# Early ring fills, a norm beside the sample index, and reordered projection openings in a two-layer decoder step

## The chip, the cores and the metric

The kernel runs on one core of a Trainium2 chip. The time is the device time of one execution in microseconds (us); 1 us is 1000 ns. Five engines run their own instruction streams: PE (matrix products and transposes; PEld is its weight load), DVE (vector work), ACT (activations, copies), POOL and SP, which here mostly issue transfers (DMA). They meet through semaphores. SBUF holds the tiles, eight banks of PSUM take PE's results.

## The reference

One inference step of two layers for a prompt of 1024 tokens and for 8 samples of 4 new tokens, each sample with 2048 past tokens in paged caches (128 tokens a page). Model width is 1024, all in float32.

```python
# layer 0: native sparse attention (compressed, selected, window) and a gated linear recurrence
y = concat([o_a * silu(z_a), o_b * silu(z_b)]) @ w_out;  x = x + gate * y
# layer 1: differential attention with a norm per head, and attention over the top 256 of an index
attn = p[..., 0, :] - lam * p[..., 1, :];  o = einsum('btghs,bsgd->btghd', attn, v)
o_c = _rmsnorm(o_c, subln_g) * (1.0 - DIFF_LAMBDA_INIT)
score = einsum('bth,bths->bts', wib * IDX_HEADS ** -0.5, relu(idx_s));  top_k(score, 256)
y = concat([o_c * silu(z_c), o_d * silu(z_d)]) @ w_out;  x = x + gate * y
```

A final RMSNorm with its own gain gives the outputs. The new key and value rows are outputs too.

## The kernel before

Each layer runs as a row of stages, and each stage is one or more blocks in which every engine has its own program; a block ends when all engines have ended. The order of the instructions on an engine is the order in which the code writes them. In each layer the stages are: norm, input projection (`project`), prompt attention (`attend_pairs`), sample attention, output projection (`output_projection`).

*Layer 0.* `nsa_prompt` begins with a small block (from line 1616) in which POOL clears a tile, ACT copies the sample rows and DVE compresses keys and values. The long attention block follows. In `nsa_sample` (line 2292) POOL fills a `Ring` of ten slots of 1 MB: 16 units of the compressed cache by indirect gather (line 2041, row numbers from the tile `rows`), ten pieces of layer 1's ada weights (line 2046), 16 units of the selected cache, 8 half units of window state and 6 more ada pieces. Before a slot is filled again POOL waits until PE has released it. DVE multiplies each compressed unit by the weights `cmp_w` (line 2354), PE sums the blocks (line 2375), copies follow (line 2341). PE multiplies ada pieces (line 350) between the steps that choose blocks, and then turns the selected keys (line 2143), scores them (line 2173) and so on, four units of four samples a half.

*Layer 1.* `diff_prompt` ends with a block for the norm per head: squares on ACT (line 1744), sums, root and scaling on DVE (lines 1754 to 1763); then `mix_prompt`: PE turns the normed rows into banks 0 to 3 (line 1578), DVE multiplies them into `mix` (line 1593). Then `sample_index`: POOL gathers 16 runs of index keys (line 2676), PE turns them in banks 5 and 6 (line 2691), ACT copies (line 2744), PE multiplies by the queries (line 2721) into banks 0 to 3, DVE rectifies (line 2785), PE sums over heads (line 2705) and DVE places the scores (line 2779). After `dsa_prompt`'s attention `layer1_sample` fills a ring of eleven slots with 16 units of diff keys, 16 of diff values and 16 of dsa keys and values, and turns and scores them as above.

*Output projection.* 18 units of 24 products (line 2894; a unit is 128 rows and one half of the columns, 512). The weights are loaded in quarters of 1 MB, two per half of the columns. ACT rounds a quarter (line 2961), DVE computes the rest (line 2908), and splits `mix` alike (lines 174, 175) for each row tile. Gates of prompt and samples are spread over partitions by PE (lines 2873, 2874) and copied by DVE (lines 2929, 2930); in layer 1 the final gain is too (lines 2880, 2935). SP loads the second half's quarters into the same room once DVE has read the first half's, and then x. The first unit's result waits for x (line 2948).

```python
                for u in range(NU):
                    ring.gather(pool, t["cmp_cache"], u)
                for n in range(m.EARLY):
                    m.fill(pool, n)
...
                split_mix(0)
                split_mix(1)
                dve.wait_ge(spread, 1)
```

## Time and profile before

| | |
|---|---|
| Median of 3 runs | 2036.73 us (2033.31 to 2038.12) |
| Profiled execution | 2032.63 us, span 2030.8 us |
| PE busy | 1759.9 us, 87% of the span |
| DVE busy | 1114.6 us, 55% |
| ACT busy | 694.5 us, 34% |
| POOL busy | 173.8 us, 9% |
| Moved by DMA | 188.68 MB, mean 93 GB/s |

The span runs from the first to the last instruction of the profiled execution. A timeline row gives start, length, engine, line, operation, output and inputs and how many instructions are merged in it; in brackets stand the idle time of that engine just before and what ended it. A wait row gives a total over a window, the number of waits and the longest. A window row gives the window, its length, busy time and instructions of PE, PEld, DVE, ACT and POOL, then the granted clock of PE as a share of full speed (2.4 GHz), the mean busy share of the DMA engines, and GB/s. `PEq`, `SPq` and `POOLq` are the engines' own sequencers; as a releaser they stand mostly for a block's end.

### The profile page before, as it was taken

The numbers are of one execution on the slowest core, as the hardware profiler recorded it, in microseconds if no ns is written. First come the engines' busy times: TensorE is split into PE (matmuls) and PEld (weight loads), VectorE is DVE, ScalarE is ACT, GpSimd is POOL, SyncE is SP. The second block draws the span as 40 slices with busy tenths as digits, with TensorE's granted clock in tenths as the row PEclk, the third lists the DMA queues.
The fourth block names the chain that finished last, engine by engine and source line by source line (L and its number), as shares of the span: only waits on it lengthen the run. The fifth ranks groups of instructions, "written<-read, shape, count | busy, mean of one in ns | idle before, by whom it ended". The sixth has DMA issues, their size and how long they took to land. (4 is left out here: it accounts for less than half of the span.)

```text
span 2030.8 us, 29356 instructions
## 1 busy us (share of the span) xinstructions
PE 1759.9 (87%) x11653; PEld 1258.7 (62%) x11653; DVE 1114.6 (55%) x2257; ACT 694.5 (34%) x1763; POOL 173.8 (9%) x212
## 2 busy tenths in 40 slices
PE   3799999699999677599899999998876999687698
PEld 2699999566666345377766766664554566444376
DVE  2445401377776733344213999943984997333454
ACT  3535521366655012211223211104662666222211
POOL 1000100000000631200000100000002000332000
PEclk9899999799999887899999999998997999899799
DMA  7411010000000993541201201100003000986221
GB/s 256 166 52 65 33 62 26 1 1 1 1 2 1 364 405 146 229 158 52 73 35 41 75 22 43 43 22 1 1 1 84 1 1 2 370 354 270 94 106 55
DMA packets 36248, 188.68 MB, mean 93 GB/s; under 512 B 5964, under 2 KB 6061, under 8 KB 19535
## 3 DMA queue, kind: packets, MB, share of 16 engines
q0 software_dynamic: 19632, 119.64, 15.1%
q1 hardware_dynamic: 16480, 67.16, 9.0%
q8 instruction: 94, 1.54, 0.3%
q14 instruction: 42, 0.34, 0.1%
HBM read 171.82 MB, written 19.12 MB: 94 GB/s over the span
## 5 line engine op out<-in xcount | busy, mean ns | idle before, releaser
L917 PE MATMUL banks<-hT,w_in 128*128 128x352 f32 x864 | 256.5, 459 | 0.0
L917 PEld LDWEIGHTS banks<-hT,w_in 128*128 128x128 f32 x864 | 164.0, 190 | 90.7
L2894 PE MATMUL banks<-w_out_parts,mix_parts 128*128 128x512 f32 (+1 forms) x864 | 202.5, 397 | 14.8 <-DVE w_out_parts L2908 10.5
L2894 PEld LDWEIGHTS banks<-w_out_parts,mix_parts 128*128 128x128 f32 (+1 forms) x864 | 158.0, 183 | 60.1 <-issue 12.1
L1529 ACT ACTIVATE nsa_p<-banks,nsa_negmax 128x512 f32<-128x512 f32 (+3 forms) x192 | 104.1, 556 | 93.9 <-DVE nsa_negmax L1446 93.9
L912 PE MATMUL banks<-hT_high,w_in_high 128*128 128x352 f32 x384 | 125.3, 326 | 0.0
L912 PE MATMUL banks<-hT_rest,w_in_high 128*128 128x352 f32 x384 | 124.0, 323 | 0.0
L912 PE MATMUL banks<-hT_high,w_in_rest 128*128 128x352 f32 x384 | 123.9, 323 | 0.0
L1446 DVE TENSOR_REDUCE nsa_negmax<-banks 128x2 f32<-128x1024 f32 (+4 forms) x77 | 84.6, 1099 | 69.5 <-PE banks L1398 59.3
L914 PE MATMUL banks<-w_in,hT 128*128 128x256 f32 (+3 forms) x576 | 117.4, 357 | 1.2 <-PEq L654 1.2
L914 PEld LDWEIGHTS banks<-w_in,hT 128*128 128x128 f32 (+1 forms) x576 | 92.2, 181 | 24.2 <-issue 10.6
L1413 PE MATMUL banks<-cf,nsa_p 128*128 128x128 f32 x544 | 77.9, 284 | 16.1 <-ACT nsa_pT L1370 13.1
L1972 DVE TENSOR_SCALAR_CACHE_REDUCE dsa_mask<-mix,prompt_top_bits 128x384 bf16<-128x384 f32 (+2 forms) x102 | 89.7, 942 | 0.6
L1413 PEld LDWEIGHTS banks<-cf,nsa_p 128*128 128x128 f32 x544 | 60.7, 145 | 36.4 <-issue 19.2
L1034 ACT ACTIVATE mix<-banks 128x352 f32<-128x352 f32 x48 | 22.2, 464 | 175.9 <-PE banks L917 91.2
L1972 DVE TENSOR_SCALAR_CACHE_REDUCE dsa_mask<-prompt_top_upper,prompt_top_bits 128x384 bf16<-128x384 bf16 (+2 forms) x90 | 79.2, 942 | 0.5
L2143 PE MATMUL banks<-cf,l_ring 128*128 128x128 f32 x384 | 61.5, 301 | 20.1 <-DMA l_ring<-in_diff_k_cache,rows 7.9
L1446 DVE TENSOR_REDUCE diff_negmax<-banks 128x2 f32<-128x1024 f32 (+3 forms) x38 | 44.3, 1165 | 60.3 <-PE banks L1398 58.8
L801 DVE TENSOR_TENSOR w_in_rest<-w_in,w_in_high 128x2048 fp32r<-128x2048 f32 (+1 forms) x10 | 23.1, 2306 | 97.4 <-ACT w_in_high L796 97.3
L907 PE MATMUL banks<-w_in_high,hT_high 128*128 128x264 f32 (+1 forms) x216 | 67.3, 312 | 8.8 <-DVE hT_rest L947 8.8
L1529 ACT ACTIVATE dsa_p<-banks,dsa_negmax 128x512 f32<-128x512 f32 (+3 forms) x96 | 54.7, 580 | 52.8 <-DVE dsa_negmax L1446 52.8
L912 PEld LDWEIGHTS banks<-hT_high,w_in_high 128*128 128x128 f32 x384 | 72.1, 188 | 0.5
(568 smaller groups left out, 3405.4 us busy)
## 6 DMA issues: line engine op xcount, KB each, us to landing
w_in<-in_w_in SPq DMA_DIRECT2D x24, 1056.0 KB, 4.9
nsa_ring<-in_ada POOLq DMA_DIRECT2D x16, 1024.0 KB, 14.7
ada_w<-in_ada SPq DMA_DIRECT2D x8, 1024.0 KB, 17.6
w_out<-in_l_w_out SPq DMA_DIRECT2D x8, 1024.0 KB, 6.7
x_in<-in_x_prompt SPq DMA_DIRECT2D x2, 2048.0 KB, 24.7
nsa_ring<-in_state_l_win_kv POOLq DMA_DIRECT2D x8, 512.0 KB, 7.5
x_after<-in_x_prompt SPq DMA_DIRECT2D x1, 4096.0 KB, 15.8
x_mid<-x_after SPq DMA_DIRECT2D x8, 512.0 KB, 2.6
```

The source lines that it names most:

```text
L801: eng.tensor_tensor(w_rest[:, j % slots, :, 0:width(j)], v, w_high[:, j % slots, :, 0:width(j)].bitcast(F32), ALU.subtract).then_inc(w_spl ...
L907: last = pe.matmul(bank[0:rows, 0:n], lhs, rhs, start=a == 0 and x == 0, stop=a == KT - 1 and x == 2)
L912: last = pe.matmul(bank[:, 0:cn], lhs, rhs, start=a == 0 and x == 0, stop=a == KT - 1 and x == 2)
L914: last = pe.matmul(bank[0:rows, 0:n], k.hT[:, a, r0:r0 + rows], w[:, j % slots, a, 0:n], start=(a == 0), stop=(a == KT - 1))
L917: last = pe.matmul(bank[:, 0:cn], w[:, j % slots, a, m * P:(m + 1) * P], k.hT[:, a, c0:c0 + cn], start=(a == 0), stop=(a == KT - 1))
L1034: act.activation(k.mix[:, what + m, c0:c0 + cn], k.bank[i % 4][:, 0:cn], ACT.Silu).then_inc(free[i % 4], 1)
L1413: last = pe.transpose(k.bank[4 + c % 2][:, i * P:(i + 1) * P], p_sb[:, u % SLOTS, col:col + P], k.const("ident"))
L1446: last = dve.tensor_reduce(of_unit(nm, u), scores_of(u), X, ALU.max, negate=True)
L1529: last = act.activation(slot_of(u)[:, g, x], scores_of(u)[:, g, x], ACT.Exp, bias=of_unit(nm, u)[:, g, x:x + 1], accum_out=of_unit(rs, u)[ ...
L1972: last = dve.tensor_scalar(m, v, threshold(j), None, op, ALU.add, accum_out=seen[:, j:j + 1])
L2143: last = pe.transpose(o[:, j * P:(j + 1) * P], ring.run[:, g % ring.slots, c % 2 * 4 + j, k_col[m]:k_col[m] + P], k.const("ident"))
L2894: last = pe.matmul(k.bank[u % 4][0:n, :], lhs, rhs, start=a == 0 and x == 0, stop=a == KT - 1 and x == 2)
```

## The change

1. The sample rings are made earlier. In layer 0 five of the ten slots lie in room that is free during the prompt attention, and POOL gathers the first five compressed units in that attention's small opening block. In layer 1 six of the eleven slots (four in the room of tensors that diff attention alone uses, two in room of their own) are filled at the start of dsa attention, with the first six units of diff keys. The sample stages fill the rest in the order as before.
2. The norm per head of diff attention, its product into `mix` and the copies of the sample rows are no longer blocks of their own. A class `DiffNorm` issues them inside `sample_index`'s block, with two tiles for squares in place of eight and three banks (2, 3, 4) in place of four.
3. In layer 1 the first half of the projection's weights is loaded by POOL as the last two fills of the ring, into the slots that the projection then reads.
4. In both output projections DVE computes the first two quarters' rests right behind the first split of `mix`; PE spreads the sample gates behind the first unit and the final gain behind the second.

```diff
--- before.py
+++ after.py
@@ -232,15 +232,23 @@
                     if layer == 0:
+                        k.ring = Ring(k, "nsa_ring", 10).add(k.sb(samples, "nsa_ring_held", [P, 5, KEYS, 2 * P], side="right"))
                         nsa_prompt(k)
                     else:
+                        k.held_stack = k.choice_stack = ExitStack()
                         diff_prompt(k)
                         dsa_prompt(k)
                 k.give_back_semaphores()
+                k.stage_sems += k.ring.filled + k.ring.free
+                if layer == 1:
+
+                    k.sb(x_stack, "w_out1", [P, 2, KEYS, 2 * P])
+                    k.w_out = k.early[:, 0:2]
...
@@ -259,10 +267,15 @@
+        k.ring = Ring(k, "l1_ring", 11)
+        k.early = k.under("l1_ring_first", [P, 4, KEYS, 2 * P], F32)
         k.qT = k.sb(st, "qcT", [P, 4, R])
+        k.kT = {n: k.sb(st, f"{n}_T1", [P, R]) for n in ("dk0", "dk1")}
+        k.v = {"dv": k.sb(st, "dv_v", [P, RT, 2 * P])}
...
@@ -1376,6 +1389,11 @@
         with nc.Block() as block:
+            if prefetch is not None:
+                @block.gpsimd
+                def _(pool):
+                    prefetch(pool)
+
@@ -1616,6 +1634,7 @@
                     pool.memset(k.qb["nsa"][:, :, :, :], 0.0).then_inc(cleared, 1)
+                    k.ring.follow(pool, nsa_items(k), 5)
...
@@ -1725,43 +1744,77 @@
         attend_pairs(k, "diff", jobs, values, close, scale, maps=True)
         with ExitStack() as ws:
...
-        mix_prompt(k, "diff", out, 0, k.lam[:, 6:7])
+            k.sample_score = k.sb(k.choice_stack, "idx_score_s", [P, QUARTER + NS], side="right")
+            sample_index(k, DiffNorm(k, ws, out))
+
+
+class DiffNorm:
+    BANKS = (2, 3, 4)
...
+    def squares(self, act):
+        for i in range(SEQ // P):
+            if i >= 2:
+                act.wait_ge(self.reduced, i - 1)
+            act.activation(self.square[:, i % 2, :], self.out[:, i, :], ACT.Square).then_inc(self.squared, 1)
...
+    def normalise(self, dve):
+        k = self.k
+        k.dve_order.link(dve, dve.tensor_scalar(k.lam[:, 6:7], k.vec[:, 8:9], 1.0 - LAM_INIT, None, ALU.mult))
+        dve.wait_ge(self.root, 1)
+        k.dve_order.link(dve, dve.reciprocal(self.ss[:, :, :], self.ss[:, :, :]))
+        for i in range(SEQ // P):
+            o = self.heads(self.out[:, i, :])
+            dve.tensor_tensor(o, o, self.ss[:, i, :].unsqueeze(2).to_broadcast([P, 4, P]), ALU.mult).then_inc(self.normalised, 1)
...
+    def turn(self, pe, u):
+        m, g = self.units[u]
+        pe.wait_ge(self.normalised, 4 * g + 4)
+        if u >= len(self.BANKS):
+            pe.wait_ge(self.taken, u - len(self.BANKS) + 1)
...
@@ -1854,10 +1907,10 @@
         with ExitStack() as ws:
-            k.sample_score = k.sb(ws, "idx_score_s", [P, QUARTER + NS], side="right")
-            sample_index(k)
             k.index_stack.close()
-            attend_pairs(k, "dsa", jobs, values, close, scale_heads, dve_copies=None, beside=SampleChoice(k, ws, k.bank[7]))
+            k.ring.add(k.early[:, 2:4]).add(k.sb(k.held_stack, "l1_ring_held", [P, 2, KEYS, 2 * P], side="right")).add(k.early[:, 0:2])
+            attend_pairs(k, "dsa", jobs, values, close, scale_heads, dve_copies=None, beside=SampleChoice(k, ws, k.bank[7]),
+                         prefetch=lambda pool: k.ring.follow(pool, layer1_items(k), 6))
...
@@ -2036,24 +2099,45 @@
+    def follow(self, pool, items, count=None):
+
+        for cache, u in items[self.issued:count]:
+            self.gather(pool, cache, u)
...
+    def load_w_out(self, pool, layer):
+        for c in range(2):
+            i = self.next(pool)
+            pool.dma_start(self.slot(i).rearrange("p i n -> p (i n)").rearrange("p (a n) -> p a n", n=512), self.k.t[f"l{layer}_w_out"].rearrange(
+                "(a p) n -> p a n", p=P)[:, c * KT // 2:(c + 1) * KT // 2, 0:512]).then_inc(self.filled[i], 16)
...
@@ -2587,12 +2671,8 @@
-                for s in range(2):
-                    for cache in ("diff_k_cache", "diff_v_cache"):
-                        for u in joint_units()[8 * s:8 * s + 8]:
-                            ring.gather(pool, t[cache], u)
-                for u in joint_units():
-                    ring.gather(pool, t["dsa_cache"], u)
+                ring.follow(pool, layer1_items(k))
+                ring.load_w_out(pool, 1)
@@ -2711,7 +2793,11 @@
                         turn(n)
+                        if n >= NU // 2:
+                            norm.turn(pe, n - NU // 2)
                     pe.wait_ge(copied, first + GROUP)
+                    if first == DB:
+                        pe.wait_ge(norm.taken, len(norm.units))
@@ -2737,11 +2823,16 @@
+                norm.squares(act)
                 for n in range(NU):
+                    if n == 4:
+                        norm.roots(act)
...
+                act.wait_ge(norm.cleared, 2)
+                keep_sample_rows(k, act, 1)
@@ -2752,6 +2843,7 @@
                 link(dve.memset(qz[:, :, :], 0.0))
+                norm.reduce(dve)
@@ -2766,6 +2858,8 @@
                 link(dve.tensor_scalar(wsum[:, :], wsum[:, :], 0.5 * HD ** -0.5, None, ALU.mult))
+                norm.normalise(dve)
+                norm.mix(dve)
@@ -2842,7 +2938,7 @@
-                for h in range(2):
+                for h in range(layer, 2):
@@ -2870,15 +2966,22 @@
                 for h in range(2):
-                    pe.matmul(k.bank[4 + h][:, :], k.const("gate_prompt"), k.gate9s[layer][:, h * 512:(h + 1) * 512], start=True, stop=True)
-                    last = pe.matmul(k.bank[6 + h][0:NS, :], k.const("gate_sample"), k.gate9s[layer][:, h * 512:(h + 1) * 512], start=True, stop=True)
+                    last = pe.matmul(k.bank[4 + h][:, :], k.const("gate_prompt"), k.gate9s[layer][:, h * 512:(h + 1) * 512], start=True, stop=True)
...
+                def beside(u):
+                    if u == 0:
+                        for h in range(2):
+                            last = pe.matmul(k.bank[6 + h][0:NS, :], k.const("gate_sample"), k.gate9s[layer][:, h * 512:(h + 1) * 512],
+                                             start=True, stop=True)
+                        last.then_inc(spread, 1)
+                    elif u == 1 and layer == 1:
...
+                    beside(u)
@@ -2923,20 +3027,22 @@
                 split_mix(0)
+                rest_of_w(0)
                 split_mix(1)
...
-                rest_of_w(0)
-                rest_of_w(1)
@@ -2957,7 +3063,10 @@
-                        act.wait_ge(loaded[h][c], 16)
+                        if h == 0 and layer == 1:
+                            k.ring.landed(act, k.ring.issued - 2 + c)
+                        else:
+                            act.wait_ge(loaded[h][c], 16)
```

On POOL, in layer 0 from the prompt attention's opening block on; `cmp_cache` is the compressed cache, `nsa_ring` the ring, `nsa_ring_held` the slots that exist early. Before, and then of the change:

```order
L1618 MEMSET nsa_qb 128x256
L154 ISA
L2041 DMA nsa_ring<-in_cmp_cache,rows 128x2048 x16
L2046 DMA nsa_ring<-in_ada 128x2048 x10
L2041 DMA nsa_ring<-in_sel_cache,rows 128x2048 x6
```

```order
L1636 MEMSET nsa_qb 128x256
L2109 DMA nsa_ring_held<-in_cmp_cache,rows 128x2048 x5
L154 ISA x2
L2109 DMA nsa_ring<-in_cmp_cache,rows 128x2048 x5
L2109 DMA nsa_ring_held<-in_cmp_cache,rows 128x2048 x5
L2109 DMA nsa_ring<-in_cmp_cache,rows 128x2048
L2114 DMA nsa_ring<-in_ada 128x2048 x4
L2114 DMA nsa_ring_held<-in_ada 128x2048 x5
L2114 DMA nsa_ring<-in_ada 128x2048
L2109 DMA nsa_ring<-in_sel_cache,rows 128x2048 x4
```

Five gathers stand ahead of the row `ISA`, which lies between the two stages; the other eleven, and all that follows them, keep their order.

On DVE, from the last copy of diff attention to the sample index's first rectified scores; `diff_ss` holds the sums of squares, `qi_z` and `wi_` rows prepare the index's queries and weights, `ki_relu` are the rectified scores. Before, and then of the change:

```order
L1724 COPY diff_out<-banks 128x512
L1754 TENSOR_REDUCE diff_ss<-diff_square 128x4 x8
L1756 TENSOR_SCALAR diff_ss<-diff_ss 128x32
L1758 TENSOR_SCALAR lam<-vec 128x1
L1760 RECIPROCAL diff_ss<-diff_ss 128x32
L1763 TENSOR_TENSOR diff_out<-diff_out,diff_ss 128x512 x8
L1593 SCALAR_TENSOR_TENSOR mix<-banks,lam,mix 128x512 x8
L2750 TENSOR_TENSOR wi_diagonal<-cf,wi 32x32 x4
L2753 MEMSET idx_score_s 96x32
L2754 MEMSET qi_z 128x256
L2760 COPY qi_z<-qiT 64x4x4 x16
L2765 TENSOR_TENSOR wi_picked<-banks,cf 128x128
L2767 TENSOR_REDUCE wi_sum<-wi_picked 128x32
L2768 TENSOR_SCALAR wi_sum<-wi_sum 128x32
L2785 TENSOR_SCALAR ki_relu<-banks 128x512 x2
```

```order
L1743 COPY diff_out<-banks 128x512
L2841 TENSOR_TENSOR wi_diagonal<-cf,wi 32x32 x4
L2844 MEMSET idx_score_s 96x32
L2845 MEMSET qi_z 128x256
L1783 TENSOR_REDUCE diff_ss<-diff_square 128x4 x8
L1785 TENSOR_SCALAR diff_ss<-diff_ss 128x32
L2852 COPY qi_z<-qiT 64x4x4 x16
L2857 TENSOR_TENSOR wi_picked<-banks,cf 128x128
L2859 TENSOR_REDUCE wi_sum<-wi_picked 128x32
L2860 TENSOR_SCALAR wi_sum<-wi_sum 128x32
L1793 TENSOR_SCALAR lam<-vec 128x1
L1795 RECIPROCAL diff_ss<-diff_ss 128x32
L1798 TENSOR_TENSOR diff_out<-diff_out,diff_ss 128x512 x8
L1817 SCALAR_TENSOR_TENSOR mix<-banks,lam,mix 128x512 x8
L2879 TENSOR_SCALAR ki_relu<-banks 128x512 x2
```

The index's preparation now stands ahead of the norm's scaling and of the product into `mix`, and the scores come behind all of it.

On DVE, at the opening of the last projection; `w_out_parts` holds the weights' two parts, `gate_rows` and `gate_rows_s` the gates, `y` a unit's result. Before, and then of the change:

```order
L174 CAST mix_parts<-mix 128x1024
L175 TENSOR_TENSOR mix_parts<-mix,mix_parts 128x1024
L174 CAST mix_parts<-mix 128x1024
L175 TENSOR_TENSOR mix_parts<-mix,mix_parts 128x1024
L2929 COPY gate_rows<-banks 128x512
L2930 COPY gate_rows_s<-banks 32x512
L2929 COPY gate_rows<-banks 128x512
L2930 COPY gate_rows_s<-banks 32x512
L2935 COPY final_g<-banks 128x512 x2
L2908 TENSOR_TENSOR w_out_parts<-w_out,w_out_parts 128x2048 x4
L2948 TENSOR_TENSOR y<-banks,gate_rows 128x512
```

```order
L174 CAST mix_parts<-mix 128x1024
L175 TENSOR_TENSOR mix_parts<-mix,mix_parts 128x1024
L3012 TENSOR_TENSOR w_out_parts<-l_ring_first,w_out_parts 128x2048 x2
L174 CAST mix_parts<-mix 128x1024
L175 TENSOR_TENSOR mix_parts<-mix,mix_parts 128x1024
L3034 COPY gate_rows<-banks 128x512 x2
L3038 COPY gate_rows_s<-banks 32x512 x2
L3012 TENSOR_TENSOR w_out_parts<-l_ring_first,w_out_parts 128x2048 x2
L3043 COPY final_g<-banks 128x512 x2
L3054 TENSOR_TENSOR y<-banks,gate_rows 128x512
```

Two of the four weight instructions moved from behind the gates and the final gain to behind the first split, and they read the ring's slots.

## Rows read from the trace of the kernel before

**Rows 1.** Window in layer 0 samples: engines' busy, PEclk, DMA share, GB/s.

```profile
674.00:742.00 68.00, 50.51 (x492) 27.58 (x492) 49.01 (x87) 4.33 (x11) 41.15 (x31) 0.89 1.01 417
```

**Rows 2.** Timeline, that stage opens: start, length, engine, line, work [idle <-releaser].

```profile
664.45 0.35 SPq L2507 DMA_DIRECT2D cmp_w<-in_cmp_w  x1
...
673.07 4.71 DVE L2354 TENSOR_TENSOR nsa_ring<-nsa_ring,cmp_w 128x2048 f32<-128x2048 f32 x2 [7.49 <-DMA nsa_ring<-in_cmp_cache,rows]
```

**Rows 3.** Tile cmp_w: from its load's issue to its landing.

```profile
DMA to landing us min/median/max: 5.3/5.3/5.3
```

**Rows 4.** Waits of PE, 717 to 742 us: total, times, longest.

```profile
PE banks L350 <- DMA nsa_ring<-in_ada: 2.0, 2, 1.4
```

**Rows 5.** Waits, 742 to 770 us, selected attention's first half.

```profile
PE banks L2143 <- DMA nsa_ring<-in_sel_cache,rows: 5.6, 4, 1.9
```

**Rows 6.** Timeline, POOL there: gathers before and beside line 2354, direct loads.

```profile
666.79 0.97 POOL L2041 DMA_INDIRECT nsa_ring<-in_cmp_cache,rows  x1 [0.30 <-issue]
...
689.57 2.23 POOL L2041 DMA_INDIRECT nsa_ring<-in_cmp_cache,rows  x1 [0.30 <-issue]
...
701.99 2.22 POOL L2046 DMA_DIRECT2D nsa_ring<-in_ada  x4
```

**Rows 7.** Timeline, the prompt attention's small opening block and what follows it.

```profile
372.75 0.31 POOL L1618 MEMSET nsa_qb<- 128x256 f32 x1 [135.40 <-POOLq L832]
...
384.05 1.22 PE L1390 MATMUL banks<-sel_T,qT 64*128 64x128 f32 x8 [4.76 <-PEq L1615]
```

**Rows 8.** Windows: norm, its product into mix, sample index.

```profile
1518.00:1530.00 12.00, 0.02 (x1) 0.06 (x1) 10.33 (x20) 8.27 (x21) 0.77 (x2) 0.66 0.00 0
1530.00:1537.50 7.50, 6.34 (x32) 6.10 (x32) 5.83 (x8) 0.00 (x0) 0.00 (x0) 0.63 0.01 2
1537.50:1569.30 31.80, 22.09 (x170) 12.18 (x170) 9.24 (x35) 9.45 (x16) 15.21 (x16) 0.79 0.48 133
```

**Rows 9.** Timeline, sample index: first gather and first turn.

```profile
1538.42 1.01 POOL L2676 DMA_INDIRECT ki_run<-in_kidx_cache,rows  x1 [19.37 <-SPq L2669]
...
1541.82 1.12 PE L2691 MATMUL banks<-cf,ki_run 128*128 128x128 f32 x4 [2.12 <-DMA ki_run<-in_kidx_cache,rows]
```

**Rows 10.** Timeline, PE, layer 1 samples: key turns, first scores, both halves.

```profile
1733.63 1.97 PE L2143 MATMUL banks<-cf,l_ring 128*128 128x128 f32 x8 [5.42 <-DMA l_ring<-in_diff_k_cache,rows]
...
1749.53 1.92 PE L2173 MATMUL banks<-l_kt,diff_qb 128*32 128x512 f32 x16
...
1785.51 3.29 PE L2143 MATMUL banks<-cf,l_ring 128*128 128x128 f32 x20
...
1796.79 1.92 PE L2173 MATMUL banks<-l_kt,diff_qb 128*32 128x512 f32 x16
```

**Rows 11.** Waits of PE, 1727 to 1750 us: total, times, longest.

```profile
PE banks L2143 <- DMA l_ring<-in_diff_k_cache,rows: 7.9, 4, 5.4
```

**Rows 12.** Timeline, opening of the last projection.

```profile
1906.33 2.04 PE L2873 MATMUL banks<-gate,cf 128*128 128x512 f32 x2 [2.73 <-PEq L2587]
...
1911.55 1.91 ACT L2961 ACTIVATE w_out_parts<-w_out 128x2048 fp32r<-128x2048 f32 x1 [7.22 <-DMA w_out<-in_l_w_out]
...
1918.53 4.49 DVE L2908 TENSOR_TENSOR w_out_parts<-w_out,w_out_parts 128x2048 fp32r<-128x2048 f32 x2
...
1920.97 23.72 PE L2894 MATMUL banks<-w_out_parts,mix_parts 128*128 128x512 f32 x96 [3.80 <-DVE w_out_parts L2908]
...
1940.75 0.69 DVE L2948 TENSOR_TENSOR y<-banks,gate_rows 128x512 f32<-128x512 f32 x1 [6.51 <-DMA x_after<-x_mid]
...
1946.73 76.72 PE L2894 MATMUL banks<-w_out_parts,mix_parts 128*128 128x512 f32 x336 [2.04 <-DVE mix_parts L175]
```

**Rows 13.** Window, first matmuls of the last projection.

```profile
1921.00:1925.00 4.00, 4.00 (x10) 3.20 (x11) 2.03 (x1) 0.00 (x0) 0.00 (x0) 0.55 0.73 246
```

**Rows 14.** Timeline, opening of the layer 0 projection.

```profile
859.00 5.81 DVE L2908 TENSOR_TENSOR w_out_parts<-w_out,w_out_parts 128x2048 fp32r<-128x2048 f32 x2 [0.39 <-ACT w_out_parts L2961]
...
888.87 6.45 PE L2894 MATMUL banks<-w_out_parts,mix_parts 128*128 128x512 f32 x20 [2.35 <-DVE mix_parts L175]
```

More of the change, by code:

```diff
@@ L446, in multiply @@
             pe.wait_ge(self.finished, 1)
-        self.columns(pe, self.bank_of(n), ring.run[:, u % ring.slots]).then_inc(self.product, 1)
+        self.columns(pe, self.bank_of(n), ring.slot(u)).then_inc(self.product, 1)
         pe.wait_ge(self.product, n + 1)
@@ L2511, in _ @@
             def _(pool):
-                for u in range(NU):
-                    ring.gather(pool, t["cmp_cache"], u)
+                ring.follow(pool, nsa_items(k)[0:NU])
                 for n in range(m.EARLY):
@@ L2671, in _ @@
             def _(pool):
+                pool.memset(k.qb["diff"][:, :, :, :], 0.0).then_inc(norm.cleared, 1)
+                pool.memset(k.qb["dsa"][:, :, :, :], 0.0).then_inc(norm.cleared, 1)
                 for n, (half, b) in enumerate(order):
```

137 lines of the change are left out of this document (78 added, 59 removed).

## The prediction

> **What bounds the kernel now.** I read the page first: TensorE (PE) is busy for 87% of the span, but that is a mean over stages. Then the windows of the five places that the change touches, the waits inside them, and the timeline where a wait ends. The prompt attentions and input projections keep PE full and move almost no data; the change adds gathers beside them and leaves their own work alone. The time to be had lies in stretches where PE waits.
>
> In layer 0's sample stage the DMA engines are the limit: from 674 to 742 us their share is 1.01 at 417 GB/s [rows 1], so 1 MB (1.049e6 bytes) lands every 2.51 us. VectorE (DVE) starts line 2354 only when the first ring units are there [rows 2], and PE still waits for ring units of ada weights and of selected keys later [rows 4, 5]. Between diff attention and dsa attention stand 51.3 us in three blocks, in none of which any engine is full [rows 8]. In layer 1's sample stage the first 16 key turns take 15.90 us where the second half's take 11.28 [rows 10]. In the last projection PE begins 14.64 us after the block does, behind the load of the weights and a queue of DVE copies [rows 12].
>
> **The change, part by part.** The sums are made against the profiled execution's own 2032.63 us (span 2030.8 and 1.8 around it), which lies 4.1 below the median of the runs shown.
>
> *Layer 0 ring, five units early.* Line 2354 now starts at 673.07, 8.6 us after the stage's load of cmp_w is issued [rows 2]. That load takes 5.3 us [rows 3] and is still needed, so the earliest new start is 664.45 + 5.3 = 669.8: 3.2 us won. With five units of 1 MB gone from a saturated stretch, 5 x 2.51 = 12.6 us of transfers are no longer ahead of the ada and selected units; the PE waits that rows 4 and 5 count, 2.0 and 5.6, lie in that backlog and should go. Sum 10.8, taken as 11. The second half of the selected attention waits for slots that the first half frees, which the change leaves, so nothing is won there. Bounds: 3.2 (only the start moves) and 12.6 (the whole of the transfers).
>
> *The gathers' new place.* In the opening block of the prompt attention POOL adds five gathers behind its memset. The block lasts from 372.75 to 384.05, 11.3 us [rows 7]. A gather takes POOL 0.97 and 0.30 to the next; beside line 2354 one took 2.23 [rows 6]. Five are then 6.4 or 12.7 us, so the block grows by 0 to 1.7. I take 0.5, nearer to the short one, since DVE works there only in the block's later part. Nothing waits for the data before the sample stage. Layer 1's six gathers open dsa attention; if each held DVE for its whole 0.97 that were 5.8, if none does 0. I take 0.5: the first of rows 2 has DVE running two instructions in 4.71 beside gathers, which is no sign of a hold.
>
> *Norm and mix beside the sample index.* Two blocks and two barriers go. The index's pipeline started with a gather at 1538.42 [rows 9]; now POOL does two memsets (its 0.77 of rows 8) and begins at about 1519.2: 19.2 us earlier. What is added to it: PE has 6.34 us of norm transposes [rows 8] between its last eight key turns, of which half fits into the gathers' period of 1.25 us (15.21 / 16 of rows 8, and 0.30); ACT does its square roots between copies; DVE can take the first rectified scores only behind the last product into mix, where before it had them ready. DVE's work in all three windows is 10.33 + 5.83 + 9.24 = 25.4 us, PE's 28.4, so neither can be full over the new stage of some 36 us. I charge 3.2 for the transposes and 1 for DVE's late turn: 15 us won. The upper bound is the 19.2. The lower one is a gather at 2.53 us all along, as beside line 2354: fifteen periods last 38.0 instead of 18.8, which eats all 19.2, and with the 4.2 above it is 4 us slower than now. I take the rows of this stage's own gathers, 15.21 us for 16, as the nearer ones, since most of DVE's work here reads the product's other input from the banks or has one input.
>
> In rows 6 the gathers go from 0.97 to 2.23 us once line 2354 runs, which reads two tiles in SBUF, while direct loads in the same stretch take 2.22 / 4 = 0.56. The Trainium skill (SBUF — State Buffer, section "Who interferes with whom") says that a DVE instruction with two SBUF inputs contends with a GpSimd instruction that reads SBUF, and infers that descriptor generation is not stopped by it. The rows agree with the first; for indirect gathers, which read their row numbers, they contradict the second. By the first statement alone only the eight normalising instructions would hold gathers up, and the sum would lose some 2 us.
>
> *Layer 1 ring, six units early.* PE waited 5.42 us before the first turn at 1733.63, so it was ready at 1728.2 [rows 10]. With the units there, 16 turns at the second half's 11.28 end at 1739.5 in place of 1749.53: 10.0 us. If PE's clock stays where it was, the turns keep 15.90 less the later waits, 7.9 - 5.42 = 2.5 [rows 11], which gives 7.9. I take 9. The remaining gathers start with the block, so units 6 and 7 land long before the third round of turns. Later waits for slots move along unchanged.
>
> *Last projection.* The first half of the weights is in the ring when the block starts at 1906.3. ACT's rounding (1.91) and one DVE split (4.49 / 2 = 2.25) follow: first quarter ready at 1910.5 where it was 1920.8, so PE starts 10.3 earlier [rows 12]. The sample gates and the final gain, two products each, move from before the units to between the first ones. One such product takes 2.04 at the low clock [rows 12] and by that 1.02 at the full one, so the four are 4.1 us more on PE there. PE lost 2.04 at the fifth unit waiting for DVE, which waited for x; x is issued behind the second quarter and moves up by 10 as well. So of the 4.1, 2.04 fill that hole: 10.3 - 4.1 + 2.0 = 8.2 won. Bounds: 10.2 (x alone sets it) and 6.2 (the hole isn't filled).
>
> *Layer 0 projection.* DVE's split waited 0.39 for ACT's rounding, which waits for its load, and PE lost 2.35 at its fifth unit [rows 14]. The reordering can't start it sooner, and the 2.0 us of gates put between units fit into the 2.35: 0, with a gain of 0.3 and a loss of 2.0 as ends.
>
> Sum: 11 + 15 + 9 + 8.2 - 0.5 - 0.5 = 42.2. The profiled execution would come to 1990.4. Other runs lie up to 5.5 above it, so for a median I add half of the 4.1: 1992.
>
> **Rivals.** *B: the gathers of the sample index are stretched by DVE for as long as it works there.* For: rows 6. Against: the 15.21 us of rows 8, where DVE was nearly idle, so it says little; and DVE's mix of instructions is another. With DVE busy 20 of the first 25 us and a gather at 2.53 in that time, 8 of 16 are stretched by 1.28 each, 10 us: 2002. Its end, all of them, is 2011.
>
> *C: the early units of layer 0 only empty the queue, and the time stays*, because DVE's own work (49.01 of 68 us in rows 1) and ten slots set the pace; only 3.2 are won. 2000. For: slots are freed by DVE and PE in pairs. Against: DMA share 1.01 with PE waiting on DMA in rows 4 and 5.
>
> *D, the slower side: PE's clock falls over part of the last projection.* Its first 10 matmuls run at a granted clock of 0.55, near the lower level of 1.2 GHz, 4.00 us or 0.40 each [rows 13]; later 336 take 76.72, or 0.228 each [rows 12]. If the new pauses between units or the earlier start kept it at the low level, each matmul would cost 0.17 more; from 42.2 / 0.17 = 248 of the 432 on, the kernel is slower than before, and with all of them it is 2065. For: the first matmuls follow a pause and start low. Against: after 4 us it was full and stayed so.
>
> **How the numbers follow.** Forecast 0.64, at 1992, its own range 1984 to 1999. B alone 0.14 (2002), C alone 0.13 (2000), both 0.05 (2010), D 0.03 (over 2036). The other 0.01 is a change without effect. Ends of the terms all at once would give 1978 and 2020; 8 in 10 lie in 1979 to 2006. A measurement of this kernel tells a difference of 0.2%, about 4 us, from none: faster 0.96, same 0.01, slower 0.03.
>
> **What would show it.** In the changed profile: line 2354's successor starts about 5.4 us into its stage, and PE's waits for ada and for selected units in the first half are gone; dsa attention starts about 36 us after diff attention's end, with gathers at 1.25 us each (near 2.5 is B); layer 1's first key turns start with the block; the first product of the last projection comes about 4.4 us after its block's start. Wrong would be: DMA waits of the same length at other lines, a gather's mean over 2 us in the sample index, or granted clocks near 0.5 in long stretches.

## The result: 22 us less in the profile where 42 were forecast

The changed kernel took 2010.73 us (median of 4 runs, 2010.16 to 2013.42), the kernel before 2035.02 beside it (2032.0 to 2038.12): a ratio of 0.9883, with an interval of 0.9864 to 0.9902. That is faster, as forecast, but 18.7 us above the 1992 of the prediction and outside its range of 1979 to 2006. The profiled executions have spans of 2030.8 and 2008.4, 22.4 less. Cut where one stage hands over to the next, the two spans give this ledger (us):

| stretch | before | after | change | forecast |
|---|---|---|---|---|
| start to layer 0's opening block | 372.8 | 373.9 | +1.2 | 0 |
| opening block of the prompt attention | 11.3 | 17.7 | +6.4 | +0.5 |
| prompt attention | 280.4 | 279.3 | -1.2 | 0 |
| layer 0 sample stage | 187.5 | 193.2 | +5.7 | -11 |
| layer 0 projection to diff attention's end | 666.3 | 664.3 | -2.0 | 0 |
| diff attention's end to dsa attention's start | 51.1 | 33.8 | -17.2 | -15 |
| dsa attention | 158.2 | 159.1 | +0.9 | +0.5 |
| layer 1 sample stage | 178.8 | 168.6 | -10.2 | -9 |
| last projection | 124.5 | 118.5 | -6.0 | -8.2 |

The whole miss is in two lines, both of layer 0's early gathers: +12.1 where -10.5 was forecast. The rest came to -34.5 in sum, forecast at -31.7.

*Opening block.* The timeline of POOL and PE after the change, against [rows 7]:

```profile
374.73 1.03 POOL L2109 DMA_INDIRECT nsa_ring_held<-in_cmp_cache,rows  x1 [0.47 <-issue]
...
380.02 0.94 POOL L2109 DMA_INDIRECT nsa_ring_held<-in_cmp_cache,rows  x1 [0.30 <-issue]
...
391.64 2.08 PE L1408 MATMUL banks<-sel_T,qT 64*128 64x128 f32 x16 [11.02 <-PEq L1633]
```

POOL's fifth gather is issued by 381, DVE's last copy ends at 385.1, yet PE's first product of the attention comes at 391.64. The windows of that time show what is still under way (the last two columns are the DMA share and GB/s):

```profile
385.00:387.00 2.00, 0.00 (x0) 0.00 (x0) 0.07 (x1) 0.00 (x0) 0.00 (x0) 0.50 1.00 422
...
389.00:390.00 1.00, 0.00 (x0) 0.00 (x0) 0.00 (x0) 0.00 (x0) 0.00 (x0) 0.50 0.59 246
...
390.00:391.60 1.60, 0.00 (x0) 0.00 (x0) 0.00 (x0) 0.00 (x1) 0.00 (x0) 0.50 0.05 20
```

No engine works; the five megabytes are still landing until about 389.8, and 1.8 us later the block ends.

*Layer 0's sample stage.* POOL's gathers after the change, against [rows 6]:

```profile
686.38 14.78 POOL L2109 DMA_INDIRECT nsa_ring_held<-in_cmp_cache,rows  x1 [7.21 <-PEq L2130]
...
701.47 0.93 POOL L2109 DMA_INDIRECT nsa_ring_held<-in_cmp_cache,rows  x1 [0.30 <-issue]
...
706.43 3.04 POOL L2109 DMA_INDIRECT nsa_ring<-in_cmp_cache,rows  x1 [0.31 <-issue]
```

One gather takes 14.78 us where POOL's others take 0.93 to 3.04. DVE in the same time, against [rows 2]:

```profile
676.08 8.90 DVE L2438 TENSOR_TENSOR nsa_ring_held<-nsa_ring_held,cmp_w 128x2048 f32<-128x2048 f32 x4 [4.08 <-DMA cmp_w<-in_cmp_w]
...
695.54 0.41 DVE L2425 COPY cmp_kv<-banks 64x256 f32<-64x256 f32 x1
...
700.27 0.41 DVE L2425 COPY cmp_kv<-banks 64x256 f32<-64x256 f32 x1
...
706.37 2.29 DVE L2438 TENSOR_TENSOR nsa_ring_held<-nsa_ring_held,cmp_w 128x2048 f32<-128x2048 f32 x1 [5.69 <-DMA nsa_ring_held<-in_cmp_cache,rows]
```

Line 2438 (2354 before) begins 5.2 us into the stage, as forecast. From 686.40 on DVE multiplies back to back, since five units more are there. The gather begun at 686.38 ends at 701.16, 0.9 us after DVE went over to a copy out of PSUM at 700.27. That copy is the last work DVE has: its ten units are used up, and the eleventh is what the held gather fetches. DVE waits 5.69 us for it, and the DMA engines, full before the change [rows 1], stand nearly idle:

```profile
686.00:702.00 16.00, 12.46 (x112) 6.80 (x112) 14.62 (x10) 0.00 (x0) 15.31 (x2) 1.00 0.20 70
```

Before the change DVE often had to wait briefly for a landing, and a gather ended some 0.8 us behind such a pause. DVE, then POOL, before:

```profile
693.85 2.29 DVE L2354 TENSOR_TENSOR nsa_ring<-nsa_ring,cmp_w 128x2048 f32<-128x2048 f32 x1 [0.18 <-DMA nsa_ring<-in_cmp_cache,rows]
...
696.36 2.29 DVE L2354 TENSOR_TENSOR nsa_ring<-nsa_ring,cmp_w 128x2048 f32<-128x2048 f32 x1 [0.22 <-DMA nsa_ring<-in_cmp_cache,rows]
```

```profile
694.46 2.49 POOL L2041 DMA_INDIRECT nsa_ring<-in_cmp_cache,rows  x1 [0.30 <-issue]
```

*The norm beside the index.* Gathers and window of the block that now holds norm, product into `mix` and sample index, against [rows 8, 9]:

```profile
1529.32 1.01 POOL L2758 DMA_INDIRECT ki_run<-in_kidx_cache,rows  x1 [0.16 <-issue]
...
1540.65 1.40 POOL L2758 DMA_INDIRECT ki_run<-in_kidx_cache,rows  x1 [0.30 <-PE banks L2773]
```

```profile
1528.30:1562.20 33.90, 25.21 (x203) 15.50 (x203) 25.79 (x63) 18.14 (x38) 16.43 (x18) 0.79 0.44 125
```

The gathers keep their period of 1.25 us; 1.40 is the longest of 16, beside the first normalising instruction. Nothing is full, and 33.8 us stand for the 51.1 before.

*Layer 1's ring and the last projection.* PE's timeline, against [rows 10, 12]:

```profile
1721.98 3.63 PE L2227 MATMUL banks<-cf,l_ring_first 128*128 128x128 f32 x16
...
1734.19 1.93 PE L2257 MATMUL banks<-l_kt,diff_qb 128*32 128x512 f32 x16
```

```profile
1894.35 8.05 PE L2997 MATMUL banks<-w_out_parts,mix_parts 128*128 128x512 f32 x24 [0.61 <-DVE w_out_parts L3012]
...
1902.34 1.91 PE L2975 MATMUL banks<-gate,cf 128*32 128x512 f32 x4
...
1909.88 1.98 PE L2982 MATMUL banks<-final_g_row,cf 1*128 1x512 f32 x4
...
1911.78 89.21 PE L2997 MATMUL banks<-w_out_parts,mix_parts 128*128 128x512 f32 x384
```

The first key turn starts with the block, and the first scores follow 12.2 us later (15.9 before, [rows 10]). In the last projection, which begins at 1889.9, the first product comes 4.4 us into the block, and from there PE never stops. Its windows, against [rows 13]:

```profile
1894.30:1898.00 3.70, 3.65 (x9) 2.91 (x10) 3.67 (x3) 0.00 (x0) 0.00 (x0) 0.50 0.72 217
...
1898.00:1904.00 6.00, 6.00 (x21) 3.58 (x19) 1.47 (x3) 2.80 (x2) 0.00 (x0) 0.89 1.04 391
...
1911.70:2000.50 88.80, 88.80 (x384) 69.34 (x384) 46.87 (x71) 9.87 (x23) 0.00 (x0) 0.98 0.11 44
```

### The profile page after: what moved, and what is told of

Its sections match the earlier page's. It is cut to its first block and busy times, and to the rows that moved or that the text cites. A ratio compares the mean times of both kernels' runs of the same rounds, so it can differ in the third digit from the quotient of the medians.

```text
span 2008.4 us, 29342 instructions
## 1 busy us (share of the span) xinstructions
PE 1761.1 (88%) x11653; PEld 1261.0 (63%) x11653; DVE 1114.5 (55%) x2257; ACT 694.6 (35%) x1763; POOL 178.5 (9%) x214
## 5 line engine op out<-in xcount | busy, mean ns | idle before, releaser
L1431 PE MATMUL banks<-cf,nsa_p 128*128 128x128 f32 x544 | 76.1, 280 | 15.9 <-ACT nsa_pT L1383 13.1
L1431 PEld LDWEIGHTS banks<-cf,nsa_p 128*128 128x128 f32 x544 | 59.2, 143 | 36.4 <-issue 20.6
L925 PEld LDWEIGHTS banks<-hT_rest,w_in_high 128*128 128x128 f32 x384 | 72.1, 188 | 0.3
```

What stands on the lines that cost most here:

```text
L925: last = pe.matmul(bank[:, 0:cn], lhs, rhs, start=a == 0 and x == 0, stop=a == KT - 1 and x == 2)
L1431: last = pe.transpose(k.bank[4 + c % 2][:, i * P:(i + 1) * P], p_sb[:, u % SLOTS, col:col + P], k.const("ident"))
```

## The experiments

Two theories were tried for the miss. Theory 1: a block doesn't end before the transfers that POOL issued in it have landed. Theory 2: a gather can't start its work while DVE multiplies with two inputs in SBUF without a pause. The spans of stretches below are cut as in the ledger, each from one profiled execution. Each ratio is to the kernel before, run beside it (2037.5 us, in the last group 2038.0).

**a1_attention: the early gathers in the long block.**

```diff
                     pool.memset(k.qb["nsa"][:, :, :, :], 0.0).then_inc(cleared, 1)
-                    k.ring.follow(pool, nsa_items(k), 5)
...
-        attend_pairs(k, "nsa", jobs, values, close, scale_heads, dve_copies=4)
+        attend_pairs(k, "nsa", jobs, values, close, scale_heads, dve_copies=4,
+                     prefetch=lambda pool: k.ring.follow(pool, nsa_items(k), 5))
```

> The five early gathers of layer 0 are issued in the long attention block, behind its start, and not in the small opening block before it. Theory 1 (a block ends only when the transfers that POOL issued in it have landed): in the changed kernel the opening block's last engine work ends at 385.1, its five megabytes land until about 389.8, and the block ends at 391.6; with the gathers in the long block it ends at about 385.4, so 6.2 us are won: 2010.7 - 6.2 = 2004.5. Rival (the opening block is longer because DVE or POOL work in it became slower): the gathers still run beside the same work or cost as much elsewhere, 2010.7. The sample stage's ring part keeps its gather of some 14.8 us in both.

Measured: 2003.61 (1998.39 to 2007.02), ratio 0.9822 [0.9787, 0.9856]. The opening block lasts 11.4 us again, and the long gather is there as before (PE's first product, POOL's gather):

```profile
385.06 2.08 PE L1408 MATMUL banks<-sel_T,qT 64*128 64x128 f32 x16 [4.75 <-PEq L1633]
...
681.37 14.78 POOL L2109 DMA_INDIRECT nsa_ring_held<-in_cmp_cache,rows  x1 [7.97 <-PEq L2130]
```

The 6.4 us go with the gathers out of the block; the attention beside them lasts 280.2, as without them (280.4 before).

**a2_attention_gap: a pause between DVE's multiplications.**

```diff
                 v = ring.slot(u)
+                if u:
+                    dve.wait_ge(weighed, u)
                 dve.tensor_tensor(v, v, wr[:, :, :], ALU.mult).then_inc(weighed, 1)
```

> As a1_attention, and DVE waits for its own multiplication before it starts the next one of line 2438, so that a short gap lies between any two. Theory 2 (a gather can't start its work while DVE runs multiplications with two SBUF inputs back to back; the gap lets it in): no gather in that stretch takes over 3 us, DVE's wait of 5.7 us for the sixth early slot's refill goes, and the ring part shortens from 55.8 us (670.9 to 726.7) to about 48: a1's time less 6 to 8, near 1998. Rival (that gather was held up by the DMA queue or by its slot): the 14.8 us stay, and sixteen gaps of 0.1 us add 1.6 to a1's time: near 2006.

Measured: 1997.77 (1992.24 to 2003.58), ratio 0.9795 [0.9757, 0.9834]. POOL, and DVE beside it:

```profile
683.33 3.10 POOL L2109 DMA_INDIRECT nsa_ring_held<-in_cmp_cache,rows  x1 [7.92 <-PEq L2130]
...
686.74 2.09 POOL L2109 DMA_INDIRECT nsa_ring_held<-in_cmp_cache,rows  x1 [0.30 <-issue]
```

```profile
688.27 4.67 DVE L2440 TENSOR_TENSOR nsa_ring<-nsa_ring,cmp_w 128x2048 f32<-128x2048 f32 x2
```

Two multiplications take 4.67 in place of 4.48, a pause of about 0.1 us between them, and the longest gather is 3.10. DVE's wait for a slot is gone, and the sample stage lasts 182.6 us. Theory 2 predicted this. The rival fails: neither queue nor slots were changed.

**a3_no_early0: no unit of layer 0 early.**

```diff
-                    k.ring.follow(pool, nsa_items(k), 5)
+                    k.ring.follow(pool, nsa_items(k), 0)
```

> The changed kernel with no unit of layer 0 gathered early (all sixteen in the sample stage, as before the change); everything else stays. If the whole loss in layer 0 (opening block 6.2, ring part 1.7 to 2.4, later parts of the stage 4.0) comes from the early gathers, the time is 2010.7 - 12 = 1998.7. If the later 4.0 us are PE's clock by chance and return in any case, 2002.7. If the early gathers had won what I forecast and the loss were elsewhere, 2021.

Measured: 2007.18 (2003.12 to 2007.41), ratio 0.984 [0.981, 0.987]: between the second and the third expectation, with an interval that overlaps that of the changed kernel. The opening block is 11.3 again, but the sample stage lasts 194.5, not 187.5:

```profile
686.07 10.04 POOL L2109 DMA_INDIRECT nsa_ring_held<-in_cmp_cache,rows  x1 [2.92 <-PEq L2130]
```

The first gather that needs a freed slot took 10.04 us here. The kernel before has one at the same place, begun at 683.97 like DVE's multiplication at 683.98; it took 5.30 and ended 0.9 after a copy:

```profile
683.97 5.30 POOL L2041 DMA_INDIRECT nsa_ring<-in_cmp_cache,rows  x1 [2.23 <-PEq L2056]
...
688.38 0.41 DVE L2341 COPY cmp_kv<-banks 64x256 f32<-64x256 f32 x1
```

So the hold was there before the change, and a stage without early units can be as long as one with them. Here it ended with the copy out of PSUM at 695.22, behind which DVE had to wait for a landing; the copy at 690.48, with the next multiplication right behind it, did not let it in, and why the like copy at 688.38 did before the change stays open. There is one profile of the kernel before, so whether 5.30 is its usual length isn't known either.

**a4_direct: plain loads in place of gathers** (of consecutive rows; the page table is left out, so this is a probe and no replacement).

```diff
         i = self.next(pool)
+        if cache is self.k.t["cmp_cache"]:
+            return pool.dma_start(self.slot(i).rearrange("p i n -> p (i n)"), page_rows(cache)[u * P:(u + 1) * P, :]).then_inc(self.filled[i], 16)
```

> The changed kernel, but the sixteen compressed units are loaded by plain loads of consecutive rows in place of indirect gathers (the same megabytes, slots and order; the rows are not those of the page table). Theory 1: the opening block still waits for its five transfers and ends some 17 to 18 us after its start. Theory 2: plain loads are not held up by DVE, so none of them takes POOL more than about 0.6 us, the hole of 5.7 us at DVE goes, and the time is 2010.7 - 8 = 2003 or less. Rivals: if the opening block ends at 385 after all, it was the gathers' own work on POOL that held it, not the landing; if DVE still finds a late slot, the 14.8 us were a matter of the queue or the slots and the time stays near 2010.

Measured: 1998.67 (1991.97 to 2005.63), ratio 0.9813 [0.977, 0.9855]. POOL, and a window at the times at which the changed kernel's DMA stood idle (4 us later in the stage here):

```profile
683.01 1.05 POOL L2110 DMA_DIRECT2D nsa_ring_held<-in_cmp_cache  x2 [12.96 <-PEq L2132]
```

```profile
686.00:702.00 16.00, 11.69 (x104) 5.99 (x102) 16.00 (x12) 0.00 (x0) 4.01 (x8) 1.00 0.99 401
```

Plain loads beside the same multiplications take 0.53 each, and DVE is busy for all of the 16.00 us. So it is the gather, not the queue or the slots, that DVE holds up. On theory 1 this run says little: the opening block lasted 16.3 us, but the small load of `cmp_w_rows` queued behind the five and DVE itself ended only at 386.6, 15.0 us in.

**b1_no_early1: no unit of layer 1 early.**

```diff
-                         prefetch=lambda pool: k.ring.follow(pool, layer1_items(k), 6))
+                         prefetch=lambda pool: k.ring.follow(pool, layer1_items(k), 0))
```

> The changed kernel with no unit of layer 1 gathered early; all else stays. By my sum the six early units are worth 9 (7.9 to 10.0), and the two profiles give 10.2 for the stage (178.9 before, 168.8 after): 2010.7 + 10 = 2020.5, with PE's wait of about 5.4 us ahead of the first key turn back. Rival (the stage is bounded by its later slots, and an early start is only waited away): no more than 3 slower, 2013.

Measured: 2016.36 (2013.66 to 2021.26), ratio 0.9907 [0.9878, 0.9937]. The stage lasts 178.6 us against 168.6, with the wait back ahead of the first key turn:

```profile
1722.52 1.97 PE L2227 MATMUL banks<-cf,l_ring_first 128*128 128x128 f32 x8 [5.71 <-DMA l_ring_first<-in_diff_k_cache,rows]
```

The 10 us of this stage are those of the six units. The median is only 5.6 above the changed kernel's where 10 were expected, and the two intervals overlap; in this profile layer 0's sample stage is the shortest of those with the same code, 187.5.

**b2_load_in_block: the last weights loaded in the block again.**

```diff
                 ring.follow(pool, layer1_items(k))
-                ring.load_w_out(pool, 1)
...
-                for h in range(layer, 2):
+                for h in range(2):
...
-                        if h == 0 and layer == 1:
-                            k.ring.landed(act, k.ring.issued - 2 + c)
-                        else:
-                            act.wait_ge(loaded[h][c], 16)
+                        act.wait_ge(loaded[h][c], 16)
```

> The changed kernel, but the first half of the last projection's weights is loaded in the projection's own block by SP again, while the new order of DVE and PE stays. If load and order each carry a part: the load takes about 5.3 us, so the first product comes 9.5 us after the block's start in place of 4.4, and the time is 2010.7 + 5 = 2015.8. If the order alone had brought the gain: 2010.7. If the load alone: the first product near 14.6 us and 2017 or more.

Measured: 2015.07 (2010.06 to 2019.54), ratio 0.9896 [0.9864, 0.9929]. PE's timeline; the block begins at 1887.4:

```profile
1897.54 8.08 PE L2996 MATMUL banks<-w_out_parts,mix_parts 128*128 128x512 f32 x24 [6.32 <-DVE w_out_parts L3011]
...
1915.00 89.19 PE L2996 MATMUL banks<-w_out_parts,mix_parts 128*128 128x512 f32 x384
```

The first product comes 10.1 us in (14.6 before), so the order does start PE 4.5 us sooner. Yet the projection lasts 124.2 us, and 124.5 before: in this profile the order alone wins nothing, since 1.90 and 1.98 of gates and gain now stand between the units and part of the products runs at a lower clock. With the new order in place the early load is worth the six microseconds (118.5); the load with the old order was not run, and the interval of the time overlaps that of the changed kernel.

**b3_norm_first: the index's gathers behind the norm.**

```diff
+                pool.wait_ge(norm.normalised, 8)
                 for n, (half, b) in enumerate(order):
...
-                    if n == 4:
+                    if n == 0:
                         norm.roots(act)
```

> The changed kernel, but in the sample index's block POOL starts its gathers only when DVE has normalised all eight tiles, and ACT takes the square roots ahead of its first copy; the same instructions, no longer beside each other. If the overlap is what won the 16.6 us between diff attention and dsa attention: the first gather comes some 14 us later than in the changed kernel, dsa attention 12 later, 2010.7 + 12 = 2022.7. Rival (two blocks and their ends fewer won it): 2010.7 + 3 or less.

Measured: 2023.2 (2017.83 to 2026.57), ratio 0.9943 [0.9923, 0.9964].

```profile
1537.54 1.01 POOL L2759 DMA_INDIRECT ki_run<-in_kidx_cache,rows  x1 [14.38 <-DVE diff_out L1798]
```

The first gather comes 15.2 us after the block's start, and the stretch from diff to dsa attention lasts 48.8 us (33.8). It is the overlap that won, and fewer blocks only the 2.3 between 48.8 and 51.1.

**b4_quarters: four short multiplications for a long one.**

```diff
-                dve.tensor_tensor(v, v, wr[:, :, :], ALU.mult).then_inc(weighed, 1)
+                for i in range(0, KEYS, 2):
+                    last = dve.tensor_tensor(v[:, i:i + 2], v[:, i:i + 2], wr[:, i:i + 2, :], ALU.mult)
+                last.then_inc(weighed, 1)
```

> The changed kernel, but each multiplication of line 2438 (128 x 2048) is written as four of 128 x 512, back to back, without a wait between them. If the end of any DVE instruction lets a gather in: no gather in this stretch lasts over 1.6 us, as beside the normalising instructions of 0.63 us in the sample index (0.95 to 1.40). If only an idle DVE, or one that reads PSUM, lets it in: the long gather stays, about 14.8 us or longer by the longer row of instructions. Four short ones for one long add some 0.2 us a unit, 3 us in all, to DVE's work.

Measured: 1999.09, one run. POOL and DVE:

```profile
681.91 6.01 POOL L2109 DMA_INDIRECT nsa_ring_held<-in_cmp_cache,rows  x1 [8.91 <-PEq L2130]
...
688.22 4.56 POOL L2109 DMA_INDIRECT nsa_ring_held<-in_cmp_cache,rows  x1 [0.30 <-issue]
...
693.08 5.11 POOL L2109 DMA_INDIRECT nsa_ring_held<-in_cmp_cache,rows  x1 [0.30 <-issue]
```

```profile
686.74 0.41 DVE L2425 COPY cmp_kv<-banks 64x256 f32<-64x256 f32 x1
...
687.07 4.89 DVE L2439 TENSOR_TENSOR nsa_ring<-nsa_ring,cmp_w 128x512 f32<-128x512 f32 x8
...
691.88 0.41 DVE L2425 COPY cmp_kv<-banks 64x256 f32<-64x256 f32 x1
```

Gathers now take 4.6 to 6.0 us. The second was issued at 688.22, in a row of eight short multiplications (687.07 to 691.96); no boundary between them let it in, and it ended at 692.78, 0.9 after the copy at 691.88. So the end of an instruction is not enough: it takes a pause, as in a2, or a copy out of PSUM, though not every copy does (after, a3). The time itself settles nothing, since one run in 1999 has its ring part no shorter (58 us to the first selected gather, as in the changed kernel) and lies within what clock and chip scatter.

**c1_changed_again, c2_gap_again, c3_weights_early, side by side.** c1 and c2 have the code of the changed kernel and of a2; c3 is c2 with

```diff
-                        k.ring = Ring(k, "nsa_ring", 10).add(k.sb(samples, "nsa_ring_held", [P, 5, KEYS, 2 * P], side="right"))
+                        held = k.sb(samples, "nsa_ring_held", [P, 5, KEYS, 2 * P], side="right")
+                        k.ring = Ring(k, "nsa_ring", 10).add(held[:, 0:4])
+                        k.cmp_w, k.cmp_w_loaded = held[:, 4], nc.alloc_semaphore("cmp_wr_loaded")
...
+        def early(pool):
+            k.ring.follow(pool, nsa_items(k), 4)
+            pool.dma_start(k.cmp_w, t["cmp_w"]).then_inc(k.cmp_w_loaded, 16)
```

> The changed kernel itself, run beside the next two on the same chip. About 0.988 of the kernel before, 2011; its long gather in layer 0's sample stage (14.8 us) and its opening block of 17.7 us are there again if they are no accident of one run. The stretch from layer 0's opening block to the first output projection lay between 486.5 and 490.6 us in the four profiles that have the same code there, by PE's clock; 479.7 before.

> a2_attention_gap again (early gathers in the long attention block, DVE waits for its own last multiplication), to measure it beside the changed kernel on one chip. By the two mechanisms 6.4 and 6 us are won: 2011 - 12 = 1999, ratio to the kernel before near 0.981.

> As c2_gap_again, but four units in place of five are gathered early and the fifth early place holds cmp_w, loaded by POOL in the long attention block; the sample stage has six slots of its own and none for cmp_w. DVE then needs nothing when the stage starts: line 2438 begins about 1 us into the stage in place of 5.4, so 4 us less than c2: 1995. Rival (the refills' landing sets the pace, not DVE's start): the same as c2; then DVE waits for the fifth or a later unit by as much as it began earlier.

Measured against 2037.98 for the kernel before: c1 2009.14, ratio 0.9855 [0.983, 0.988], with the long gather again (14.77) and an opening block of 18.0; the stretch from opening block to projection was 494.5, above the expected bounds. c2 1994.43, ratio 0.979 [0.9765, 0.9815]. c3 1990.5, ratio 0.9763 [0.9732, 0.9794]. c2 and c3 beat the changed kernel; between the two the intervals overlap. DVE in c3 starts 1.0 us into the stage:

```profile
666.06 9.47 DVE L2448 TENSOR_TENSOR nsa_ring_held<-nsa_ring_held 128x2048 f32<-128x2048 f32 x4
```

Its first selected gather comes 48.0 us into the stage, in c2 52.0. In the profiled execution, c3's slowest (1997.34), the 4 us were lost again behind it, most of them in the selected attention's first half, c3 first, then c2:

```profile
731.40:768.50 37.10, 26.45 (x238) 16.93 (x239) 10.91 (x20) 9.31 (x22) 3.25 (x3) 0.71 0.58 241
```

```profile
732.20:766.00 33.80, 22.98 (x234) 14.77 (x234) 10.91 (x20) 9.37 (x22) 3.28 (x2) 0.85 0.57 235
```

The granted clock there was 0.71 against 0.85. Whether c3 is faster than c2 stays open.

**c4_two_in_opening: two early gathers in the opening block, three behind it.**

```diff
-                    k.ring.follow(pool, nsa_items(k), 5)
+                    k.ring.follow(pool, nsa_items(k), 2)
...
+                     prefetch=lambda pool: k.ring.follow(pool, nsa_items(k), 5))
```

> The changed kernel, but two of the five early gathers stand in the opening block and three at the start of the long attention block. If the block waits for the landing of what was issued in it: two megabytes land within 9 us of the first gather, before DVE ends at about 11.2 us, and the block lasts 11.4 us as before the change. If each gather in the block costs a share of the 6.4 us: 2.6 us more, 13.9.

Measured: 2002.41, one run. The opening block begins at 372.11:

```profile
383.85 2.08 PE L1408 MATMUL banks<-sel_T,qT 64*128 64x128 f32 x16 [4.76 <-PEq L1633]
```

It lasts 11.7 us: two gathers cost at most 0.4 where five cost 6.4. Theory 1 holds, a price per gather does not.

## Why the prediction was wrong, point by point

- *Five units early.* This step failed: "five units of 1 MB gone from a saturated stretch" were to take 11 us off, 3.2 by an earlier start and 7.6 by PE waits that should go. The start came as forecast. But over the seven profiles with the changed kernel's multiplications and five early units (after, a1, b1, b2, b3, c1, c4) the stage lasts 187.5 to 196.3 us, 192.9 on average, 5.4 more than before. What it had wrong is the pace of the stage and what PE's waits hang on:
  - The saturated DMA was read as the pace-maker, but DVE's own work was as slow. From its first multiplication of line 2354, at 673.07 [rows 2], to the copy behind its last one DVE takes 40.9 us before the change, with some 2 us of short waits for landings in them; the same work takes 40.7 in c2. The copy before, then both ends in c2:

```profile
713.55 0.41 DVE L2341 COPY cmp_kv<-banks 64x256 f32<-64x256 f32 x1
```

```profile
669.27 9.49 DVE L2440 TENSOR_TENSOR nsa_ring_held<-nsa_ring_held,cmp_w 128x2048 f32<-128x2048 f32 x4 [4.09 <-DMA cmp_w<-in_cmp_w]
...
709.55 0.41 DVE L2425 COPY cmp_kv<-banks 64x256 f32<-64x256 f32 x1
```

  - It was in those short waits that POOL's gathers got in. With data at hand they go, DVE shuts the gathers out (14.8 us), and the DMA engines fall to a share of 0.20. From its start to the first selected gather the stage takes 57.4 to 59.5 us in the seven, 55.6 before, and 52.2 and 52.0 with pauses (a2, c2): the hold costs some 6 us. I had seen gathers stretched by line 2354 in [rows 6] and weighed it as a rival for the sample index, where it didn't happen, and not for the stage from which the rows came; that trace also has the gather of 5.30, which [rows 6] leave out.
  - PE's 7.6 us of waits [rows 4, 5] did not all lie in that backlog. In the changed kernel 1.5 for ada and 4.1 for selected units are left; without the hold the ada waits are gone, and 5.1 of the 5.6 for selected units stay (c2):

```profile
PE banks L2227 <- DMA nsa_ring<-in_sel_cache,rows: 3.0, 2, 1.9
PE banks L2227 <- DMA nsa_ring_held<-in_sel_cache,rows: 2.1, 2, 1.8
```

  - Behind the first selected gather the stage takes 129.0 to 136.9 us in the seven, 134.6 on average, and 131.9 before, at granted clocks of 0.74 to 0.81 and with the same busy time of DVE, ACT and POOL. So half of the 5.4 lies there, and that it comes from the hold isn't shown.
- *What was to be had there.* Without the hold (a2, c2) the stage lasts 182.6 and 182.2, 5 us less than before, not 11. Of that 3.4 and 3.6 lie ahead of the first selected gather, where rival C gave 3.2, for the reason it gave: DVE's own work is the pace. The other 1.4 and 1.7 are within the spread of the part behind. No run has the pauses without early units, so how much of the 5 each brings stays open.
- *The gathers' new place.* Failed too: "Nothing waits for the data before the sample stage" left out the block itself, which waits for what was issued in it. 6.4 us in place of 0.5 (a1, c4). The DVE part was right: 1.2 us of multiplication lasted 1.22 beside the gathers.
- *Norm beside the index.* 17.2 for 15, by the overlap (b3). The gathers began 19.2 sooner, as forecast, and of the 4.2 charged to PE and DVE 2.0 were paid. Rival B fell: the gathers kept 0.95. What makes the eight normalising instructions harmless, whose second input is spread from four numbers a row, isn't settled; that they are short isn't it (b4).
- *Layer 1's ring.* 10.2 for 9, by the units (b1); the upper bound of 10.0 was right.
- *Last projection.* 6.0 for 8.2. Start (10.2 sooner, 10.3 forecast) and gates (3.9 for 4.1) were right, and the hole of 2.04 is gone. PE's products and gates took 106.64 us where the working gives 100.4 + 3.9 = 104.3; the 2.3 are clock: 0.89 for 6 us after the start and 0.98 over the last 89, where the kernel before had 1.00 behind its first 4 us. Rival D's mechanism in small.
- *Layer 0 projection.* 2.0 for 0 over the whole stretch, all of it in the projection; 0.45 is the hole filled, the rest clock.
- *Range and rivals.* The ends "all at once", 1978 and 2020, don't follow from the terms: their own ends add up to gains of 52.3 and 3.8 us, or 1982 and 2031 for the median. B and C together had 2010, which is what came, but by luck: B did not occur.

The Trainium skill (SBUF — State Buffer, section "Who interferes with whom") states that a DVE instruction with two SBUF inputs contends with a GpSimd instruction that reads SBUF; the traces agree (14.78 us beside such multiplications, 0.94 without). It infers that such instructions leave descriptor generation alone. The gather of 14.78 us, against plain loads at 0.53 and gathers with pauses at 3.10, says otherwise for indirect gathers.

## What to carry to other kernels

Before work is brought forward, ask what the waiting engine's pauses let through: here a wait of DVE's was what kept POOL's gathers moving. A transfer issued early belongs into a block that outlasts its landing, or the block waits for it. A full DMA share doesn't show that transfers set the pace: here the engine that used the data was as slow, its row of work took 40.9 us before and 40.7 without the hold, and only its earlier start could be won.

## What the runs showed of the hardware

- A gather issued beside back-to-back two-input multiplications lasted 14.77 to 14.78 us in all seven profiles with that code, until DVE had no unit left; with pauses of about 0.1 us between them gathers lasted at most 3.51 (a2, c2, c3). Held gathers end 0.8 to 1.2 us after DVE pauses or turns to a copy out of PSUM; not every such copy lets them in.
- A block with five gathered megabytes ended 1.8 us after the last of them had landed (after); with two it ended with its engines, 0.3 us after DVE's last copy (c4).
- PE's granted clock moves one and the same code by several us: the last 16 to 21 us of layer 0's sample stage took 16.0 at a mean clock of 1.00 (a4) and 20.6 at 0.76 (a1):

```profile
828.20:844.20 16.00, 10.42 (x147) 5.74 (x146) 6.51 (x17) 4.21 (x12) 4.42 (x5) 1.00 0.64 262
```

```profile
839.90:860.50 20.60, 13.77 (x147) 7.04 (x145) 6.51 (x17) 4.21 (x12) 4.43 (x5) 0.76 0.52 204
```
